# A decoder step on one core: adaLN weights moved into the norms, routing in another order, the last expert's result straight into the residual

## The reference

```
cs = silu(c)
for l in (0, 1):
    sh1, sc1, gt1, sh2, sc2, gt2 = split(cs @ w_ada[l] + b_ada[l], 6)
    h = rmsnorm(x, norm_mix[l]) * (1 + sc1) + sh1
    x = x + gt1 * mixer(h)        # 4 GLA heads and 4 gated-delta heads, then @ w_out
    h = rmsnorm(x, norm_ffn[l]) * (1 + sc2) + sh2
    f = swiglu(h) if l == 0 else moe(h)      # 2816 wide; 8 experts, 3584 wide
    x = x + gt2 * f
y = rmsnorm(x, norm_final) * (1 + scf) + shf

def moe(h):
    top_v, top_i = top_k(h @ w_router, 2)
    combine = softmax(top_v) placed at top_i
    return sum over e of combine[e] * swiglu(h, expert e)
```

## Time and profile before

| what | value |
|---|---|
| median of 3 runs | 2044.63 us |
| the profiled execution | 2043.25 us, of which its span is 2041.5 |
| TensorE busy | 1903.1 us (93% of the span) |
| VectorE busy | 1450.5 us (71%) |
| ScalarE busy | 1101.1 us (54%) |
| HBM read | 494.88 MB, 247 GB/s over the span |
| mean granted clock of TensorE | 0.953 |

### The profile page before, as it was taken

The page is one execution under the profiler, slowest core; times in us unless marked ns, Lnnn a source line. Parts: engine busy times, 40 slices in busy tenths (PEclk is TensorE's granted clock), DMA queues, the critical chain, the costliest instruction groups (busy, mean ns, idle before and its releaser), DMA issues.

```text
span 2041.5 us, 25178 instructions
## 1 busy us (share of the span) xinstructions
PE 1903.1 (93%) x10264; PEld 1566.4 (77%) x10264; DVE 1450.5 (71%) x1771; ACT 1101.1 (54%) x1101; POOL 12.7 (1%) x27
## 2 busy tenths in 40 slices
PE   5997998899989978986999999999999999999995
PEld 3995666899989956665878787787887877878783
DVE  3847647655348666475878788787888888878884
ACT  3744232333237543223667676676766767667672
POOL 0000000000000000000000000000000000000000
PEclk8997799899999978985999999999999999999998
DMA  9445374343353453731889899998998989989880
GB/s 382 149 137 179 114 271 158 123 146 125 128 182 118 147 175 117 261 143 62 321 327 361 316 355 338 330 358 319 348 345 325 362 320 341 350 324 356 335 321 27
DMA packets 92119, 505.29 MB, mean 248 GB/s; under 512 B 8064, under 2 KB 8224, under 8 KB 40544
## 3 DMA queue, kind: packets, MB, share of 16 engines
q1 hardware_dynamic: 89616, 488.29, 65.0%
q0 software_dynamic: 2384, 15.34, 2.0%
HBM read 494.88 MB, written 8.72 MB: 247 GB/s over the span
## 4 chain that ended last, share of the span: by engine, by line
issue 56%; PE 30%; DVE 11%; ACT 2%; SPq 1%; DMA 1%; POOL 0%; DVEq 0%; ACTq 0%; POOLq 0%
PE bank L610 29%; DVE wlo L424 2%; DVE work L1706 1%; SPq L524 1%; DMA raw<-in_w_in 1%; ACT L1241 1%; DVE wscr L1858 1%; PE bank L834 1%; DVE work L1707 1%; ACT work L1241 1%; DVE wscr L1930 0%; ACT whi L419 0%; DVE hT L1620 0%; DVE hl L1628 0%; DVE work L1838 0%
## 5 line engine op out<-in xcount | busy, mean ns | idle before, releaser
L424 DVE TENSOR_TENSOR wlo<-raw,whi 128x2048 fp32r<-128x2048 f32 (+1 forms) x412 | 920.1, 2262 | 211.1 <-ACT whi L419 209.6
L419 ACT ACTIVATE whi<-raw 128x2048 fp32r<-128x2048 f32 (+1 forms) x412 | 761.5, 1889 | 80.6 <-PE bank L610 75.4
L610 PE MATMUL bank<-whi,hg_high 128*128 128x512 f32 x896 | 368.7, 412 | 1.5 <-DVE hg_low L2121 1.5
L610 PE MATMUL bank<-whi,hg_low 128*128 128x512 f32 x896 | 354.8, 396 | 0.0
L610 PE MATMUL bank<-wlo,hg_high 128*128 128x512 f32 x896 | 354.7, 396 | 0.0
L610 PE MATMUL bank<-hh,whi 128*128 128x320 f32 x944 | 299.3, 317 | 24.3 <-DVE hl L1628 18.2
L610 PE MATMUL bank<-hh,wlo 128*128 128x320 f32 x944 | 293.9, 311 | 0.0
L610 PE MATMUL bank<-hl,whi 128*128 128x320 f32 x944 | 293.6, 311 | 0.0
L1241 ACT ACTIVATE work<-bank 128x512 f32<-128x512 f32 (+3 forms) x217 | 101.3, 487 | 277.4 <-PE bank L610 247.9
L610 PEld LDWEIGHTS bank<-hh,whi 128*128 128x128 f32 x944 | 180.0, 191 | 32.8 <-issue 23.4
L610 PEld LDWEIGHTS bank<-whi,hg_high 128*128 128x128 f32 x896 | 168.9, 188 | 43.1 <-issue 4.4
(11 more groups left out here) (259 smaller groups left out, 1883.0 us busy)
## 6 DMA issues: line engine op xcount, KB each, us to landing
raw<-in_moe SPq DMA_DIRECT2D x336, 1024.0 KB, 4.8
raw<-in_ada SPq DMA_DIRECT2D x56, 1024.0 KB, 5.3
raw<-in_w_in SPq DMA_DIRECT2D x30, 1024.0 KB, 4.8
raw<-in_gu SPq DMA_DIRECT2D x22, 1024.0 KB, 4.8
raw<-in_down SPq DMA_DIRECT2D x16, 704.0 KB, 4.0
raw<-in_w_out SPq DMA_DIRECT2D x8, 1024.0 KB, 5.0
work<-in_s_gdn POOLq DMA_DIRECT2D x2, 2048.0 KB, 12.6
out_gdn_s<-work POOLq DMA_DIRECT2D x2, 2048.0 KB, 7.4
```

The lines of the kernel that those rows point to most:

```text
L419: ac.activation(whi[:, part(n), 0:width(n)], raw[:, n % SLOTS, 0:width(n)], ACT.Copy).then_inc(S("w_high"), 1)
L424: ve.tensor_tensor(wlo[:, n % SLOTS, 0:width(n)], raw[:, n % SLOTS, 0:width(n)], whi[:, part(n), 0:width(n)], ALU.subtract).then_inc(S("w_ ...
L610: return pe.matmul(out, lhsT, rhs, start=start, stop=stop, **k)
```

## The change

- SP's order of loads is written out as a list (`ring_order`, `RING`), in which sets 3 and 4 stand among the chunks of `gu` and of the second `w_in`. Each slot and landing count follows from the list.
- Set 3 is multiplied behind `sum_squares` of norm 2 in layer 0 (chunks 0 to 5) and after units 1 and 2 of gate and up (6 and 7), and turned after unit 4. Set 4 lies in the same way in norm 1 of layer 1 and after units 3 and 4 of its projection, turned after unit 6. Mixer 1 keeps one set, 5. Set 6 lies in norm 2 of layer 1 (0 to 5) and in routing (6 and 7).
- VectorE's split of a further weight chunk ahead of norm 2 is left out in both layers, and two of ScalarE's splits ahead of norm 1 of layer 1 are made behind it.
- Routing: eight products of 8 by 320 for the logits, turned back by three small transposes; one ranking over 192 elements; tokens turned by halves of the width into five banks; the one-hot matrix ahead of most of `htok_low`; combine weights, `flag` and the clearing of `hT` behind the gathers; `ada_turn(6)` between the gathers and `turn_gathered`.
- The last expert: the sum of the first seven is added to `xT` beside its products (eight calls of `residual`), and its own result goes from the bank into `xT`. `flag` is read ahead of the scatter. In the branch for overflow `hT` is cleared and added by code of its own.
- `y` is stored in four transfers of 320 KB, each when its two slices are written, with no `y_done`.

```diff
+def ring_order():
+    def ada(x, *ks):
+        yield from (("ada", x, k) for k in ks)
+    def weights(first, n):
+        yield from (("w", first + i) for i in range(n))
+    yield from ada(0, *range(KD))
+    yield from weights(AT_IN[0], H_IN)
+    yield from ada(1, *range(KD))
+    yield from ada(2, *range(KD))
+    yield from weights(AT_OUT[0], H_OUT)
+    for x, first, n in ((3, AT_GU, H_GU + H_DN), (4, AT_IN[1], H_IN)):
+        yield from ada(x, 0)
+        yield from weights(first, 1)
+        yield from ada(x, 1, 2, 3, 4, 5)
+        yield from weights(first + 1, 3)
+        yield from ada(x, 6, 7)
+        yield from weights(first + 4, n - 4)
+    yield from ada(5, *range(KD))
+    yield from weights(AT_OUT[1], H_OUT)
+    yield from ada(6, *range(KD))
+    yield from weights(AT_MOE, len(MOE))
...
+                    if l and u in (3, 4):
+                        ada(4, u + 3)
+                    if l and u == 6:
+                        ada_turn(4)
...
-                ada_turn(x + 1)
+                if l == 0:
+                    ada_turn(2)
                 heads_spread(("heads", 2 * l + 1))
                 after(pe, "gdn_state", l, 1)
                 new_values(1)
-                ada(x + 2, 0)
                 keys(2)
-                ada(x + 2, 1)
                 after(pe, "do", l, 1)
                 outputs(1)
-                ada(x + 2, 2, 3)
                 new_values(2)
...
+                ada((3, 6)[l], 0, 1, 2, 3, 4, 5)
                 if l == 0:
...
+                        if u in (1, 2):
+                            ada(3, u + 5)
+                        if u == 4:
+                            ada_turn(3)
...
+                    ada(4, 0, 1, 2, 3, 4, 5)
...
-                for i, (t0, nt) in enumerate(TILES):
-                    ins = mm(B[0][0:nt, NE * i:NE * (i + 1)], hT[:, k, t0:t0 + nt], wrt[:, k, :], k == 0 and i == 0, k == KD - 1,
-                             skip_group_check=True)
+                ins = mm(B[0][0:NE, 0:T], wrt[:, k, :], hT[:, k, :], k == 0, k == KD - 1)
             ins.then_inc(S("logits_mm"), 1)
+            def turn_tokens(u):
+                c, i = u // 3, u % 3
+                t0, nt = TILES[i]
+                for k in range(4):
+                    ins = pe.transpose(B[2 + u % 5][0:nt, k * P:(k + 1) * P], hT[:, 4 * c + k, t0:t0 + nt], ident)
+                ins.then_inc(S("htok_tr"), 1)
+            turn_tokens(0)
+            pe.wait_ge(S("logits_row"), 1)
             for i, (t0, nt) in enumerate(TILES):
-                for c in range(2):
-                    u = 2 * i + c
-                    if u >= 2:
-                        pe.wait_ge(S("htok"), u - 1)
-                    for k in range(4):
-                        ins = pe.transpose(B[2 + u % 2][0:nt, k * P:(k + 1) * P], hT[:, 4 * c + k, t0:t0 + nt], ident)
-                    ins.then_inc(S("htok_tr"), 1)
+                ins = pe.transpose(B[1][0:nt, NE * i:NE * (i + 1)], rt[0:NE, t0:t0 + nt], ident[0:NE, 0:NE])
+            ins.then_inc(S("logits_tr"), 1)
+            turn_tokens(1)
+            turn_tokens(2)
             pe.wait_ge(S("sel"), 1)
             for i in range(3):
                 for j in range(i + 1):
                     rows = TILES[j][1]
-                    m = TILES[i][1]
-                    lhsT = cst("strict", rows)[:, 0:m] if j == i else ones[0:rows, 0:m]
-                    mm(B[1][0:m, NE * i:NE * (i + 1)], lhsT, sel[0:rows, NE * j:NE * (j + 1)], j == 0, j == i)
+                    lhsT = cst("strict", rows) if j == i else ones[0:rows, :]
+                    mm(B[1][:, NE * i:NE * (i + 1)], lhsT, sel[0:rows, NE * j:NE * (j + 1)], j == 0, j == i)
             for j in range(3):
                 rows = TILES[j][1]
                 ins = mm(B[1][:, 32:32 + NE], ones[0:rows, :], sel[0:rows, NE * j:NE * (j + 1)], j == 0, j == 2)
             ins.then_inc(S("pos_mm"), 1)
-            pe.wait_ge(S("htok"), 6)
+            turn_tokens(3)
+            turn_tokens(4)
+            pe.wait_ge(S("htok"), 1)
+            turn_tokens(5)
+            ada(6, 6, 7)
...
+                pe.wait_ge(S("htok"), 3 * c + 3)
                 gather(0, c, B[4 + c]).then_inc(S("e_gather_mm"), 1)
+            ada_turn(6)
...
+                    high.to(AT_IN[l])
...
-                        low.to(AT_OUT[l] + j // 2 + 2)
+                    if j % 2 and j < KD - 1:
+                        low.to(min(AT_OUT[l] + j // 2 + 2, AT_OUT[l] + H_OUT - l))
...
+            do(cp(rt[0:NE, :], B[0][0:NE, 0:T]), "logits_row")
             ve.wait_ge(S("vec_own"), own.n["vec_own"])
-            go(cp(LG[:, 0:16], B[0][:, 0:16]))
-            do(cp(LG[0:TS, 16:24], B[0][0:TS, 16:24]))
+            ve.wait_ge(S("logits_tr"), 1)
...
+            token_low(0)
+            token_low(1)
+            ve.wait_ge(S("pos_mm"), 1)
+            pos3 = v3(pos[:, :], 3)
+            sel3, cw3 = v3(sel[:, :], 3), v3(cw[:, :], 3)
+            do(stt(pos3[:, :, 0:NE], sel3, -FAR, v3(B[1][:, 0:3 * NE], 3), ALU.mult, ALU.add))
+            do(ts(pos3[:, :, 0:NE], pos3[:, :, 0:NE], FAR, None, ALU.add))
+            def onehot(col):
+                for i, (t0, nt) in enumerate(TILES):
+                    ins = ts(ONEH[0:nt, i, :], cbf("iota", nt), pos3[0:nt, i, col], None, ALU.is_equal)
+                return ins
+            onehot(slice(0, 1)).then_inc(S("onehot"), 1)
+            for u in range(2, 6):
+                token_low(u)
+            low.to(AT_MOE + 1)
+            ada_add(6)
...
+            ve.wait_ge(S("htok_tr"), 6)
+            do(ve.memset(hT[:, :, :], 0.0), "flag_ready")
...
+                if e == NE - 1 and c in (3, 4) and (kind, b) in SPREAD:
+                    j = 4 * (c - 3) + SPREAD.index((kind, b))
+                    ve.wait_ge(S("e_scatter"), KD * (NE - 1))
+                    residual(hT[:, j, :], j, 48 + 40, None)
...
+            more = ve.value_load(flag[0:1, 0:1], min_val=0, max_val=1)
             for j in range(KD):
-                ve.wait_ge(S("e_sc_mm"), KD * (NE - 1) + j + 1)
-                scattered(j, B[4 + j % 2]).then_inc(S("e_scatter"), 1)
-            ve.wait_ge(S("e_scatter"), KD * NE)
-            more = ve.value_load(flag[0:1, 0:1], min_val=0, max_val=1)
+                n, bank, gate = KD * (NE - 1) + j + 1, B[4 + j % 2], md(48 + 40)
+                xs = v3(xT[:, j, TP:], NSEQ)
+                ve.wait_ge(S("e_sc_mm"), n)
+                go(stt(xT[:, j, 0:TP], bank[:, 0:TP], gate[:, j, 0:1], xT[:, j, 0:TP], ALU.mult, ALU.add))
+                tt(v3(rt[:, 0:TS], NSEQ), v3(bank[:, TP:T], NSEQ), last(gate[:, j, 1:], LSEQ), ALU.mult).then_inc(S("e_scatter"), 1)
+                ve.wait_ge(S("e_scatter"), n)
+                do(tt(xs, xs, v3(rt[:, 0:TS], NSEQ), ALU.add), "x_moe")
...
-            po.wait_ge(S("y_done"), 1)
-            store(O["y"], hT[:], "y_out")
+            po.wait_ge(S("hs_norm"), 5)
+            for k in range(1, KD, 2):
+                po.wait_ge(S("h_norm"), KD + k + 1)
+                store(O["y"][:, k - 1:k + 1, :], hT[:, k - 1:k + 1, :], "y_out")
```

More of the change, by code:

```diff
@@ L334, in build @@
         FSG = [rs[:, :], rv[:, :]]
-        AROW = w(WORK + TD - CH, CH)
+        AROW = [w(WORK - CH if x in (3, 4, 6) else WORK + TD - CH, CH) for x in range(N_ADA)]
         CBF = w(KD * P, N_CB)
@@ L1191, in _ @@
                     beside(at_e, at_c, kind, b)
+            more = pe.value_load(flag[0:1, 0:1], min_val=0, max_val=1)
             pe.wait_ge(S("e_y"), NE)
```

260 lines of the change are left out of this document (132 added, 128 removed).

## The result

The changed kernel took 2033.04 us (median of 5 runs, 2032.28 to 2034.88), the kernel before beside it 2044.47. The ratio is 0.9948, 95% interval 0.9937 to 0.9959: faster by 11.4 us, where 26 had been forecast. The time lies 2 us above the stated range.

A forecast was written before the change was run, and what follows sets the result against it. TensorE was taken to bound the experts and gate and up, VectorE the norms. Terms summed to -26.3 us from the profiled 2043.25, giving 2017.0, median 2018; 8 in 10: 2007 to 2031 us.

The forecast's parts named there:

- Projection of layer 1: +3: Second projection: 2.4 us more products, late fifth `w_in` chunk delaying VectorE's splits, 0.6 for `ada_add(4)`; +3 us, between +1 and +5.
- Gate and up, +2.3: Gate and up: two set chunks and the turn cost their full time on TensorE, +2.3 us; bound 3.5 if chunk 6 is late.
- The rival on the loads: New ring stalls both projections: 5 us in the projection, 3 in gate and up beyond the terms; 2025 us, chance 0.08.
- norm 2 of layer 0: Norm 2, layer 0: VectorE's split gone saves 1.4 us, TensorE's kept clock 0.9, six chunks hidden; -2.3 us.
- norm 1 of layer 1: Norm 1, layer 1: 5.6 us of set products fit into a 6.10 us stretch without any; 0.
- mixer 0: Mixer 0: loses one set, the part behind the inversion, with its turn and addition; -4.4 us, bounds 3 to 6.
- mixer 1: Mixer 1: loses the part behind the inversion and eight chunks beside the inversion; -8.2 us, bounds 6 to 10.5.
- The rival that the mixers keep their time: Mixers: chunks lie in waits and the clock falls without them; they give 3 instead of 12.6 us, 2028 us, chance 0.16.
- Routing, -11.5: Norm 2 and routing, layer 1: shorter logits, earlier prefix sum and gathers, start experts near 958.5; -11.5 us, bounds -8 to -14.5.
- the tail (+2.2): Routing, layer 1: the way from gather to first expert product takes 5.7 us, not 3.5; +2.2 us.
- The end, -5.5: End: residual beside scatter products and `flag` read gives 3 us, four smaller stores without a sign 2.5; -5.5 us.
- The forecast of the experts: Experts: 24 more VectorE instructions in the last expert, beside products, with VectorE having time to spare; +0.3 us.

The follow-up runs named there:

- e1_ring: Changed kernel with the first weight chunk of gate and up and of the second projection loaded behind four set chunks instead of one: 2027.56 us, ratio 0.9924.
- e6_turn: Changed kernel with three edits for set 4: load order, ScalarE's copy earlier, VectorE's addition earlier with the decay sums later: 2016.15 us, ratio 0.9869.
- e7_thin: Changed kernel with set 6's first six chunks multiplied over 8 of 512 columns only: 2033.29 us, ratio 0.9958.
- e3_tail: Kernel before with only the change of the end (early residual, four stores, `flag` read ahead of the scatter): 2039.21 us, ratio 0.9978.
- e12_sums: e6_turn with TensorE's sums of squares at the end placed between scatter products and ahead of the branch: 2011.11 us, ratio 0.9845.
- e8_both: Changed kernel with set 4 back in mixer 1 and the first gate and up chunk loaded behind four chunks of set 3: 2017.24 us, ratio 0.9872.
- e2_rows: Changed kernel with ScalarE's copy of set 4's sums ahead of unit 4's weight split: 2027.31 us, ratio 0.9918.
- e5_set4: Changed kernel with set 4 moved back into mixer 1 and set 5 beside the inversion: 2018.13 us, ratio 0.9875.

## Why the prediction was wrong

**The failed step is "Projection of layer 1: +3".** It measured +15.5, and these 12.5 us are most of the 15.6 by which the profiled execution missed the forecast (-10.7 for -26.3). The step said that a late fifth chunk makes VectorE's splits late, that TensorE has 1.4 us of room, and that `ada_add(4)` takes 0.6 more. The late load was right, though the reason given for it was not: the two set chunks' slots were free, and the load of the fourth `w_in` chunk ahead of them held the queue, so that this chunk was late too (ScalarE waited 6.3 us for the two). But no `wlo` was late for TensorE. I had priced the turn and the addition as work, a few tenths of a microsecond each, and never asked what each is queued behind. Three things followed. TensorE asks for the turn after unit 6, when ScalarE, one to two units behind by design with four banks between them, has still to do unit 5 (3.6 us, e1_ring). Bank 6 is held until VectorE's addition, and the wait for it, `pe.wait_ge(S("ada_done"), 5)` ahead of the sums for the decay, is one line of the change that my step doesn't mention (2.85 us). And both waits were followed by a stretch at 1.2 GHz, 5.1 and 5.9 us long, of which half, 5.5 us together, is lost. With the waits removed the clock stayed at 1.00 (e6_turn). I had counted the clock in the mixers and not where a stall was possible.

**Gate and up, +2.3, upper bound 3.5, measured +6.1.** The mechanism that I kept as a bound came true, and e1_ring took off 3.6: 2.0 of waiting and 1.7 for the clock behind it. The rival on the loads had both places and a chance of 0.08; it asked for 5 and 3 us beyond my terms, and the loads were worth 3.1 and 3.6 (e1_ring). The chance was too low, since the ring's rule (a load waits for the chunk eight places earlier) could have been followed in the list: the slot of the first `w_in` chunk goes to the fourth.

**Down, +1.5, forecast 0.** In both traces TensorE waits 1.94 us at its start. After this wait it ran at 1.2 GHz for 3.4 us in the changed kernel and not in the kernel before; nor in e7_thin, where down took 82.63. Nine more kernels with set 3 moved have this stretch, e3_tail without the move has not. So it goes with the change in all but one, and why is not shown.

**Right in size:** norm 2 of layer 0 (-2.1 for -2.3), norm 1 of layer 1 (0), mixer 0 (-4.1 for -4.4) and mixer 1 (-7.2 for -8.2). The rival that the mixers keep their time fell. From the last product of the projection to the first of the output projection mixer 1 is at a granted clock of 0.83, over the same stretch before at 0.87. That agrees in kind with the rule of the Trainium skill ("TensorE: Matmul & The Clock Gate", "What's actually happening") that spoke against emptying the mixers, but the products removed weighed more.

**Routing, -11.5, measured -15.0.** The order was right, and so were the logits, the prefix sum and the tail (+2.2). What was mis-sized is the clock in between: the turns and set chunks behind the prefix sum were over 1.2 us sooner than my sum has them, and the gathers, which I let run as slowly as before (5.8 us in my sum), took 3.6 at full clock.

**The end, -5.5, measured -5.0.** The stores gave 1.5, not 2.5: the last 320 KB landed 3.3 us after its issue. The estimate of 2.75 from the Trainium skill ("DMA: Bandwidth & Descriptors", "Anatomy of one DMA") was 0.5 too low. From the first issue at 2022.78 to the last landing there were 5.4 us, so the four overlap and don't pay the fixed part four times. The early residual gave the other 3.5, where 3 had been forecast. Its last slice was ready 9.9 us earlier, counted from the last expert product, and the place of the sums of squares behind the scatter and the branch took most of that (e12_sums). The end of one and the same instructions took 29.5 us (e8_both) to 33.2 (e2_rows), of it the sums of squares 4.6 and 7.6 by their clock, so the 0.5 us by which the forecast missed say nothing. The forecast of the experts missed 0.8 us of clock at their start.

**Two sums.** The rival on the loads, 5 and 3 us on top of 2018, is 2026, not 2025. The bounds of the terms as written add up to about 2006 to 2032, not 2004 to 2033.

**Not settled:** the first projection, whose instructions no kernel changed, took 110.4 us in some profiled executions (after, e5_set4) and 111.9 in others (before, e6_turn). Both kinds begin with some us at 1.2 GHz (before 3.8, after 5.7); the longer ones have 3.4 us more of it some 65 us later. What decides that I have not tried to find.

## What to carry to other kernels

When an operation is moved into an engine's queue, price what it waits for and not only what it takes: list, for each engine on its way, how many units that engine is behind at that point, and for each buffer that it holds, who needs the buffer next. In an in-order ring, follow every load to the use that frees its slot before you trust that "it is loaded in a gap". And price a new wait of TensorE above its own length, for the slow clock that may follow. In this case 9 us of waits brought 5.5 more, while single waits of 1.8 to 2.1 us brought 1.7 us or nothing.

## What the runs showed of the hardware

- A wait of TensorE of 1.94 us at the same place (start of down) was followed by 3.4 us at 1.2 GHz in the changed kernel and by none in the kernel before. In gate and up a wait of 2.02 us for a load was followed by 3.4 us at 1.2 GHz in the changed kernel, one of 1.81 in e7_thin by none. Waits of 2.85 and 6.11 us (changed kernel) and 5.8 (e2_rows) were followed by it. Among single profiled executions, stages of the same instructions so differed by 1.5 us (82.63 and 84.15; experts 1034.9 and 1036.3), and the end by 3.7 (29.5 and 33.2).
- Three edits on the way of one set, which has two linked waits of TensorE, gave 3.1, 3.3 and 5.6 us alone and 13.8 together.
- Four stores of 320 KB from GpSimd's queue, issued 0.5 to 0.8 us apart, overlapped: median 3.0 us each to landing, all landed 3.3 us after the last issue.
